# GpSimd's modulation units pause in parts of the last two layers, and three smaller edits on TensorE

## The chip, the cores and the metric

The kernel runs on one core of one Trainium2 chip. The metric is the device time of one execution in microseconds. TensorE's clock has two levels, 1.2 and 2.4 GHz; the profile shows the granted one as a share of the higher, so 0.50 is 1.2 GHz. All data is float32.

## What is computed

Two blocks of two layers each work on a sequence of 256 positions with 2048 features. The first block has a convolution and latent attention layer and a grouped attention layer. The second block, in which most of this change lies, is this, once for each of its two layers (cut to what matters):

```python
for l in range(2):
    shift, scale, gate = jnp.split(c_act @ w_ada[l] + b_ada[l], 3, axis=-1)
    h = rms_norm(x, norm_w[l]) * (1.0 + scale[:, None, :]) + shift[:, None, :]
    (gq, gk, gv, glr, gz, dq, dk, dv, da, db, dz, aq, ak, av, az) = jnp.split(h @ w_in[l], bounds, axis=-1)
    # gated linear attention, 4 heads of 64 key and 128 value features, in chunks of 64 positions
    att = jnp.where(causal, jnp.einsum('bhncd,bhnsd->bhncs', q_e, k_e), 0.0)
    o_gla = jnp.einsum('bhncs,bhnsv->bhncv', att, v) + jnp.einsum('bhncd,bhndv->bhncv', q_e, s_prev)
    # gated delta rule: its q, k and v pass a convolution over 4 positions first
    qkv = jax.nn.silu(causal_depthwise_conv(jnp.concatenate([dq, dk, dv], axis=-1), gdn_conv_w[l]))
    # differential attention, 8 query and 8 key maps of 128 features
    q_d = rms_norm(aq.reshape(B, S, 4, 2, 128), diff_q_norm_w[l])
    k_d = rms_norm(ak.reshape(B, S, 4, 2, 128), diff_k_norm_w[l])
    x = x + gate[:, None, :] * (jnp.concatenate([o_gla, o_gdn, o_diff], axis=-1) @ w_out[l])
```

The modulation vectors (shift, scale, gate) are products of one row with a matrix of 2048 x 6144 in each of the four layers; in the first block they are wanted for two rows, the input's and the context's.

## The kernel before

The large weights stream through the chip as 346 tiles of 128 output features by 2048 input features, 1 MB each. SyncE issues their loads (`load`, L724), four tiles ahead, into a ring of four buffers. Every tile is split into two parts for accuracy: ScalarE rounds it to an upper part (`upper`, L862), VectorE subtracts to get the lower part (`lower`, L1461), and TensorE then does 48 matmuls of 128x128 by 256 columns on it (`part_of_tile`, L2385): high by high, high by low, low by high, for each of 16 steps, in two halves of 8 steps. ScalarE copies the result out (L875).

The tiles are numbered through the whole program. The input tiles of layer 2, the first of the second block, are 194 to 253 (phase `s_in2`), its output tiles 254 to 269 (`s_out2`); layer 3 has 270 to 329 (`s_in3`) and 330 to 345 (`s_out3`). Between the phases stand the norms, which must be ready before the next tile can start. The small work of a layer (norms, linear attention, delta rule, differential attention) is written as one generator per engine; it is cut into pieces by slot numbers, two slots for a weight tile, and each piece stands in the engine's instruction order behind that half of a tile. Every engine works strictly in its order.

The tiles of `dq`, `dk` and `dv` have the convolution: for each, VectorE does one scaling (L2214) and three multiply-adds over 128x256 (L2216), besides the lower half of the weight tile.

The modulation vectors are worked out beside the weight tiles, in 80 blocks of 256 features. 24 blocks, 192 units, belong to TensorE: their pieces of weight go to three buffers (`load_gemv`), and `gemv_units` does them. A table, `GEMV_AT`, gives for each tile in the first block a list of up to three units: the first two of the list stand in the middle of the tile, a third behind it. Sixteen tiles have three. The other 56 blocks are GpSimd's, four units each. A unit is a load of 512 KB (`load_pool`, L722), which SyncE issues right behind the load of a weight tile, and six GpSimd instructions (L819 twice, L822, L826 or L828, L829). `pool_units_by(q)` gives how many units are issued by the load of tile q: two for every three tiles from tile 97 on. When a block is finished TensorE transposes its row (L2348), VectorE or ScalarE takes it in (`mod_event`), and `MOD_COLS_AT` gives the tile. `gains(l)` works out products of the scale vectors with the norm's weights.

Linear attention's outputs, at slot `gla_o`, are made head by head (L2751 and L2755): for one head four chunks, the first term with the full height of the array, the second with 64 rows, the lower half of the rows for one head of a pair and the upper half for the other. Even heads write bank G[2], odd ones G[3]. At slot `diff_qs`, TensorE sums the squares of the queries with 16 matmuls of one result column each (L2887), and those of the keys with `row_sums`, eight matmuls that leave their sums as rows (L2554).

## Time and profile before

| | us |
|---|---|
| Median of three runs | 2895.1 |
| The three runs | 2896.65, 2884.96, 2895.1 |
| The profiled execution | 2885.66 |
| Its span | 2882.8 |
| TensorE busy | 2724.0 (94%) |
| VectorE busy | 1739.1 (60%) |
| ScalarE busy | 1208.2 (42%) |
| GpSimd busy | 1476.2 (51%) |
| Mean granted TensorE clock | 0.969 |

### The profile page before, as it was taken

The numbers are of one execution on the slowest core, as the hardware profiler recorded it, in microseconds if no ns is written. First come the engines' busy times: TensorE is split into PE (matmuls) and PEld (weight loads), VectorE is DVE, ScalarE is ACT, GpSimd is POOL, SyncE is SP. The second block draws the span as 40 slices with busy tenths as digits, with TensorE's granted clock in tenths as the row PEclk, the third lists the DMA queues.
The fourth block names the chain that finished last, engine by engine and source line by source line (L and its number), as shares of the span: only waits on it lengthen the run. The fifth ranks groups of instructions, "written<-read, shape, count | busy, mean of one in ns | idle before, by whom it ended". The sixth has DMA issues, their size and how long they took to land.

```text
span 2882.8 us, 51276 instructions
## 1 busy us (share of the span) xinstructions
PE 2724.0 (94%) x22179; PEld 2516.7 (87%) x22179; DVE 1739.1 (60%) x1903; ACT 1208.2 (42%) x1438; POOL 1476.2 (51%) x1071
## 2 busy tenths in 40 slices
PE   5799999999999999999999969899999898999999
PEld 2488888888888899889989959899899798999999
DVE  2343544654554658686677665965766658745753
ACT  1233444333333334344575364532453445434442
POOL 0056766976676787665436826544548754400000
PEclk8799999999999999999999979999999998999999
DMA  9998998998887988776556837755668676644465
GB/s 337 292 309 254 275 265 243 290 285 246 242 240 227 288 246 225 202 208 183 156 142 187 236 95 189 208 153 140 176 163 219 184 198 172 165 112 122 121 164 155
DMA packets 948768, 599.21 MB, mean 208 GB/s; under 512 B 22070, under 2 KB 945088, under 8 KB 948032
## 3 DMA queue, kind: packets, MB, share of 16 engines
q1 hardware_dynamic: 944720, 582.83, 72.3%
q10 hardware_dynamic: 3824, 13.11, 1.2%
q8 instruction: 175, 2.87, 0.4%
q14 instruction: 49, 0.40, 0.0%
HBM read 589.46 MB, written 6.29 MB: 207 GB/s over the span
## 4 chain that ended last, share of the span: by engine, by line
PE 74%; DVE 12%; DMA 6%; ACT 3%; POOL 2%; issue 2%; SPq 1%; DVEq 0%; ACTq 0%; POOLq 0%
PE G L2385 55%; DMA ring<-in_w_mod_dram 3%; DVE ring_r L1461 3%; PE A L2325 2%; DMA const<-in_w_mod_dram 1%; DVE S L2216 1%; PE A L2447 1%; PE A L2453 1%; POOL ring L819 1%; PE A L2450 1%; PE G L2469 1%; PE A L2488 1%; ACT ring_r L862 1%; PE G L2824 1%; PE A L2836 1%
## 5 line engine op out<-in xcount | busy, mean ns | idle before, releaser
L2385 PE MATMUL G<-H_r,ring_r 128*128 128x256 f32 x10032 | 1706.6, 287 | 54.0 <-DVE S_r L1450 19.7
L2385 PEld LDWEIGHTS G<-H_r,ring_r 128*128 128x128 f32 x10032 | 1476.5, 191 | 90.1 <-issue 61.2
L819 POOL TENSOR_TENSOR ring<-ring,act_in 128x512 f32<-128x512 f32 x448 | 673.2, 1523 | 979.5 <-DMA ring<-in_w_ada_dram 736.6
L1461 DVE TENSOR_TENSOR ring_r<-ring,ring_r 128x2048 fp32r<-128x2048 f32 x346 | 860.7, 2488 | 287.3 <-ACT ring_r L862 286.2
L862 ACT ACTIVATE ring_r<-ring 128x2048 fp32r<-128x2048 f32 x346 | 661.6, 1912 | 325.7 <-PE G L2385 104.0
L2385 PE MATMUL G<-M_r,ring_r 128*128 128x256 f32 x4528 | 788.9, 284 | 0.0
L2385 PEld LDWEIGHTS G<-M_r,ring_r 128*128 128x128 f32 x4528 | 643.8, 189 | 12.0 <-issue 11.4
L2385 PE MATMUL G<-S_r,ring_r 128*128 128x256 f32 x1920 | 550.3, 287 | 0.0
L2385 PEld LDWEIGHTS G<-S_r,ring_r 128*128 128x128 f32 x1920 | 373.9, 195 | 3.4 <-issue 3.4
L822 POOL TENSOR_TENSOR ring<-ring 128x512 f32<-128x512 f32 x224 | 362.0, 1616 | 17.6
L828 POOL TENSOR_TENSOR ring<-ring 128x256 f32<-128x256 f32 x168 | 204.1, 1215 | 13.2
L829 POOL TENSOR_TENSOR mod_rows<-mod_rows,ring 128x256 f32<-128x256 f32 x168 | 183.3, 1091 | 13.2
L875 ACT ACTIVATE S<-G 128x256 f32<-128x256 f32 (+1 forms) x138 | 52.9, 384 | 282.3 <-PE G L2385 282.1
L2325 PE MATMUL A<-const,act_in 128*32 128x256 f32 x768 | 73.6, 394 | 13.4 <-DMA const<-in_w_mod_dram 12.9
L1680 DVE SCALAR_TENSOR_TENSOR X<-G,mod,X 128x256 f32<-128x256 f32 x80 | 38.4, 481 | 68.4 <-PE G L2385 67.9
L875 ACT ACTIVATE M<-G 128x256 f32<-128x256 f32 x72 | 27.4, 381 | 102.9 <-PE G L2385 102.9
L2295 PE MATMUL G<-ring,act_in 128*32 128x256 f32 x512 | 46.6, 527 | 23.4 <-DMA ring<-in_w_mod_dram 23.4
L1504 DVE TENSOR_REDUCE small<-G 128x2 f32<-128x256 f32 x44 | 18.5, 421 | 76.5 <-PE G L2348 76.3
L875 ACT ACT_TABLE_LOAD x43 | 55.2, 1283 | 19.3 <-PE G L2385 18.6
L2216 DVE SCALAR_TENSOR_TENSOR S<-M,pcol,S 128x256 f32<-128x256 f32 x72 | 59.8, 831 | 2.6
L1580 DVE TENSOR_REDUCE small<-G 128x1 f32<-128x256 f32 (+1 forms) x32 | 17.7, 554 | 69.2 <-PE G L2473 69.2
L1113 ACT ACTIVATE E<-G,small 128x512 f32<-128x512 f32 x32 | 24.9, 779 | 75.9 <-DVE small L1784 75.8
(440 smaller groups left out, 2611.9 us busy)
## 6 DMA issues: line engine op xcount, KB each, us to landing
ring<-in_w_in_dram SPq DMA_DIRECT2D x120, 1024.0 KB, 5.7
ring<-in_a_w_in_dram SPq DMA_DIRECT2D x98, 1024.0 KB, 7.0
ring<-in_w_ada_dram SPq DMA_DIRECT2D x192, 512.0 KB, 6.8
const<-in_w_mod_dram SPq DMA_DIRECT2D x192, 256.0 KB, 5.5
ring<-in_c_w_in_dram SPq DMA_DIRECT2D x48, 1024.0 KB, 5.8
ring<-in_w_mod_dram SPq DMA_DIRECT2D x16, 2048.0 KB, 18.0
ring<-in_a_w_out_dram SPq DMA_DIRECT2D x32, 1024.0 KB, 6.5
ring<-in_w_out_dram SPq DMA_DIRECT2D x32, 1024.0 KB, 5.9
```

Source lines behind the costliest of these rows:

```text
L819: g.mark(pool.tensor_tensor(w[:, i:i + 2, :], w[:, i:i + 2, :], act_in[:, k:k + 2, c:c + 1].broadcast_to((P, 2, BW)), ALU.mult))
L822: g(pool.tensor_tensor(w[:, 0:2, :], w[:, 0:2, :], w[:, 2:4, :], ALU.add))
L828: g(pool.tensor_tensor(w[:, 0, :], w[:, 0, :], w[:, 1, :], ALU.add))
L829: ins = pool.tensor_tensor(total, total, w[:, 0, :], ALU.add)
L862: act.activation(w_up(tl), w_raw(tl), ACT.Copy).then_inc(w_hi, 1)
L875: act.activation(dst, G[tl.bank][0:rows, 0:SEQ], func).then_inc(bank_free[tl.bank], 1)
L1461: v.tensor_tensor(w_low(tl), w_raw(tl), w_up(tl).bitcast(F32), ALU.subtract).then_inc(w_lo, 1)
L1680: v.scalar_tensor_tensor(out=x[:, j, :], in0=G[tl.bank][:, 0:SEQ], scalar=mod[:, gate:gate + 1], in1=x[:, j, :], op0=ALU.mult, op1=ALU.add ...
L2216: ins = v.scalar_tensor_tensor(out=CA[:, j % 2, :], in0=src, scalar=w, in1=CA[:, j % 2, :], op0=ALU.mult, op1=ALU.add)
L2295: ins = pe.matmul(G[2 * (b % 2)][o:o + 32, 0:BW], act_in[:, k, :], wide(b % 4)[:, k, :], start=(k < 4), stop=(k >= KT - 4))
L2325: ins = pe.matmul(A[3][o:o + 32, 0:BW], act_in[:, k, :], gemv_unit(m)[:, i, :], start=(k < 4), stop=(k >= KT - 4), skip_group_check=True)
L2385: ins = pe.matmul(G[tl.bank][:, 0:SEQ], w, x, start=(k == 0 and n_ == 0), stop=(k == KT - 1 and n_ == 2))
```

## The change

1. `pool_units_by` leaves out the load tiles in `PAUSED`: in each of the two layers those from four tiles ahead of its first input tile to one behind it, and those of the tiles 9 to 24. The rate in other tiles is 18 for every 25 instead of 2 for 3, and the last unit's load stands with tile 328 instead of 298. Through the later blocks, `gains(3)` moves behind output tile 11 of layer 2.
2. The sums of squares of the queries are made with `row_sums` as rows of 256, the root, reciprocal and scaling work on 128x256, and two transposes and a copy bring them into the former place.
3. Linear attention's outputs are looped over pairs of heads, positions and then the two heads of the pair.
4. `gemv_units` does the whole list in the middle of the tile.

```diff
+PAUSED = [FIRST[_name][0] + _j for _name in ("s_in2", "s_in3") for _j in [*range(-4, 2), *range(9, 25)]]
 def pool_units_by(q):
     first = max(0, min(q, 97) - 7)
-    return min(POOL_UNITS, first + 2 * max(0, q - 97) // 3)
+    working = max(0, q - 97) - sum(97 < p <= q for p in PAUSED)
+    return min(POOL_UNITS, first + 18 * working // 25)
...
-                    take_root(f"diff_q{l}", small[:, 32:48])
+                    take_root(f"diff_q{l}", df["q_rows"])
...
-                    ask_root(f"diff_q{l}", small[:, 32:48], G[3][:, 0:16], 1.0 / P)
-                    V(v.reciprocal(small[:, 32:48], small[:, 32:48]))
-                    V(v.tensor_scalar(small[:, 32:48], small[:, 32:48], P ** -0.5, None, ALU.mult))
+                    q_rows = df["q_rows"]
+                    ask_root(f"diff_q{l}", q_rows, G[3][:, 0:SEQ], 1.0 / P)
+                    V(v.reciprocal(q_rows, q_rows))
+                    V(v.tensor_scalar(q_rows, q_rows, P ** -0.5, None, ALU.mult))
...
                     after_p("diff_bc", l)
+                    turned_q = G[3][:, SEQ:2 * SEQ].rearrange("p (t g x) -> p t g x", t=2, g=4)
+                    V(v.tensor_copy(small[:, 32:48].rearrange("p (t g r) -> p t g r", t=2, g=4), turned_q[:, :, :, 0:2]))
...
-                if l == 2:
-                    gains(3)
                 for j in range(16):
...
                     mod_event(FIRST[f"s_out{l}"][0] + j)
+                    if l == 2 and j == 11:
+                        gains(3)
...
-                gemv_units(GEMV_AT.get(q, [])[0:2])
+                gemv_units(GEMV_AT.get(q, ()))
...
-                        else:
-                            gemv_units(GEMV_AT.get(q, [])[2:])
...
-                    for h in range(GLA_H):
-                        p, b, o = h // 2, h % 2, 64 * (h % 2)
-                        for c in range(NCH):
-                            t = c // 2
-                            if c % 2 == 0:
+                    for p in range(2):
+                        for t in range(2):
+                            for b in range(2):
+                                h = 2 * p + b
                                 pe.matmul(G[2 + b][:, p * SEQ + t * P:p * SEQ + (t + 1) * P], GV[:, t, h * P:(h + 1) * P],
...
+                            for c in range(max(1, 2 * t), 2 * t + 2):
+                                for b in range(2):
+                                    o = 64 * b
+                                    ins = pe.matmul(G[2 + b][:, p * SEQ + c * CHUNK:p * SEQ + (c + 1) * CHUNK],
...
-                    for j in range(8):
-                        for t in range(2):
-                            ins = pe.matmul(G[3][:, t * 8 + j:t * 8 + j + 1], df["sq_q"][:, j, t * P:(t + 1) * P], ones[:, 0:1],
-                                            start=(j == 0 and t == 0), stop=True, skip_group_check=True)
+                    ins = row_sums(None, [(j // 2, j % 2, df["sq_q"][:, j, :]) for j in (0, 2, 4, 6, 1, 3, 5, 7)], G[3], SEQ)
...
+                    for t in range(2):
+                        pe.transpose(G[3][:, SEQ + t * P:SEQ + (t + 1) * P], df["q_rows"][:, t * P:(t + 1) * P], ident)
```

SyncE's order in layer 3 before, where the convolution tiles' weights are loaded; `in_w_in` is a weight tile, `in_w_ada` a GpSimd unit's piece:

```order
L722 DMA ring<-in_w_ada_dram 128x4x256
L729 DMA ring<-in_w_in_dram 128x16x128
L722 DMA ring<-in_w_ada_dram 128x4x256
L729 DMA ring<-in_w_in_dram 128x16x128 x2
L722 DMA ring<-in_w_ada_dram 128x4x256
```

The same stretch in the changed kernel, from the last loads of layer 2's output tiles on:

```order
L734 DMA ring<-in_w_out_dram 128x16x128 x4
L734 DMA ring<-in_w_in_dram 128x16x128 x4
L727 DMA ring<-in_w_ada_dram 128x4x256
L734 DMA ring<-in_w_in_dram 128x16x128
L727 DMA ring<-in_w_ada_dram 128x4x256
L734 DMA ring<-in_w_in_dram 128x16x128
L727 DMA ring<-in_w_ada_dram 128x4x256
L734 DMA ring<-in_w_in_dram 128x16x128 x2
L727 DMA ring<-in_w_ada_dram 128x4x256
L734 DMA ring<-in_w_in_dram 128x16x128
L727 DMA ring<-in_w_ada_dram 128x4x256
L734 DMA ring<-in_w_in_dram 128x16x128 x18
```

A unit's load behind every tile or every second one is gone from two stretches, of 8 and of 18 weight loads.

TensorE's order at the linear attention outputs before, the first two heads; G2 and G3 are the banks, E and H the inputs of the first term, X and S those of the second:

```order
L2751 MATMUL G2<-E,H 128x128
L2755 MATMUL G2<-X,S 128x64
L2751 MATMUL G2<-E,H 128x128
L2755 MATMUL G2<-X,S 128x64 x2
L2751 MATMUL G3<-E,H 128x128
L2755 MATMUL G3<-X,S 128x64
L2751 MATMUL G3<-E,H 128x128
L2755 MATMUL G3<-X,S 128x64 x2
```

And in the changed kernel, the same two heads:

```order
L2756 MATMUL G2<-E,H 128x128
L2756 MATMUL G3<-E,H 128x128
L2762 MATMUL G2<-X,S 128x64
L2762 MATMUL G3<-X,S 128x64
L2756 MATMUL G2<-E,H 128x128
L2756 MATMUL G3<-E,H 128x128
L2762 MATMUL G2<-X,S 128x64
L2762 MATMUL G3<-X,S 128x64
L2762 MATMUL G2<-X,S 128x64
L2762 MATMUL G3<-X,S 128x64
```

The same matmuls stand in another order, with the bank changing at each one, and fewer changes between the two terms.

TensorE's order at the first modulation units before; L2325 is a unit of the modulation, two instructions each, L2385 the weight tile:

```order
L2325 MATMUL A<-const,act_in 32x256 x4
L2385 MATMUL G<-H_r,ring_r 128x256 x24
L2325 MATMUL A<-const,act_in 32x256 x2
L2385 MATMUL G<-H_r,ring_r 128x256 x24
L2325 MATMUL A<-const,act_in 32x256 x4
L2385 MATMUL G<-H_r,ring_r 128x256 x24
L2325 MATMUL A<-const,act_in 32x256 x2
L2385 MATMUL G<-H_r,ring_r 128x256 x24
```

And in the changed kernel, where the lines are L2333 and L2393:

```order
L2333 MATMUL A<-const,act_in 32x256 x6
L2393 MATMUL G<-H_r,ring_r 128x256 x48
L2333 MATMUL A<-const,act_in 32x256 x6
L2393 MATMUL G<-H_r,ring_r 128x256 x48
L2333 MATMUL A<-const,act_in 32x256 x4
```

The third unit, which stood between two tiles, has moved half a tile forward.

## Rows read from the trace of the kernel before

**Rows 1.** The page's list of busy times and their share of the span.
```profile
PE 2724.0 (94%) x22179; PEld 2516.7 (87%) x22179; DVE 1739.1 (60%) x1903; ACT 1208.2 (42%) x1438; POOL 1476.2 (51%) x1071
```
**Rows 2.** Timeline of TensorE in a weight tile: start us, length us, instruction.
```profile
2480.09 0.28 PE L2385 MATMUL G<-S_r,ring_r 128*128 128x256 f32 x1
...
2480.80 0.28 PE L2385 MATMUL G<-S_r,ring_r 128*128 128x256 f32 x1
```
**Rows 3.** Windows: length, busy time of five engines, clock, DMA share, GB/s.
```profile
1786.00:1872.00 86.00, 78.28 (x659) 75.39 (x658) 79.26 (x79) 47.11 (x55) 42.63 (x36) 0.98 0.79 212
2386.00:2480.00 94.00, 83.87 (x686) 81.13 (x685) 83.02 (x80) 49.72 (x57) 51.48 (x38) 0.95 0.72 191
```
**Rows 4.** TensorE's waits from 1780 to 1870: total us, times, longest.
```profile
PE G L2385 <- ACT M L875: 3.3, 1, 3.3
PE G L2348 <- ACT M L875: 2.5, 1, 2.5
PE G L2385 <- DVE mod L1436: 1.9, 2, 1.7
```
**Rows 5.** TensorE's waits from 2390 to 2480.
```profile
PE G L2385 <- DVE mod L1441: 5.6, 2, 3.2
PE G L2385 <- ACT M L875: 4.6, 1, 4.6
```
**Rows 6.** Timeline of VectorE in the convolution tiles of layer 3.
```profile
2441.27 2.29 DVE L1461 TENSOR_TENSOR ring_r<-ring,ring_r 128x2048 fp32r<-128x2048 f32 x1 [1.79 <-ACT ring_r L862]
...
2443.86 1.53 DVE L2216 SCALAR_TENSOR_TENSOR S<-M,pcol,S 128x256 f32<-128x256 f32 x3
...
2453.82 3.13 DVE L1461 TENSOR_TENSOR ring_r<-ring,ring_r 128x2048 fp32r<-128x2048 f32 x1
...
2458.04 3.23 DVE L2216 SCALAR_TENSOR_TENSOR S<-M,pcol,S 128x256 f32<-128x256 f32 x3
```
**Rows 7.** TensorE at the linear attention outputs: timeline, then a clock window.
```profile
1742.43 1.16 PE L2721 MATMUL G<-X 64*128 64x128 f32 x16
...
2372.13 0.39 PE L2751 MATMUL G<-E,H 128*128 128x128 f32 x2
...
2379.44 1.11 PE L2755 MATMUL G<-X,S 64*128 64x64 f32 x4
...
2377.40:2384.20 6.80, 6.80 (x28) 0.50 0.00 0
```
**Rows 8.** Query norms: TensorE and VectorE timelines, then a clock window.
```profile
2642.98 3.63 PE L2887 MATMUL G<-ones,H 128*128 128x1 f32 x32
...
2654.95 1.14 PE L2685 MATMUL A<-S,const 32*128 32x256 f32 x16
...
2458.82 1.07 PE L2554 MATMUL A<-E,small 128*32 128x256 f32 x16
...
2649.84 1.75 DVE L1920 RECIPROCAL S<-S 128x256 f32<-128x256 f32 x1 [0.55 <-ACT S L1198]
...
2647.00:2650.50 3.50, 3.50 (x24) 0.51 0.32 76
```
**Rows 9.** Modulation units: TensorE's timeline, the page's group and DMA line.
```profile
566.56 0.79 PE L2325 MATMUL A<-const,act_in 128*32 128x256 f32 x8
...
570.31 0.63 PE L2325 MATMUL A<-const,act_in 128*32 128x256 f32 x4
...
L2325 PE MATMUL A<-const,act_in 128*32 128x256 f32 x768 | 73.6, 394 | 13.4 <-DMA const<-in_w_mod_dram 12.9
...
const<-in_w_mod_dram SPq DMA_DIRECT2D x192, 256.0 KB, 5.5
```
**Rows 10.** Windows over the same stretch of layer 2 and of layer 3.
```profile
1891.70:2181.60 289.90, 285.07 (x2297) 271.86 (x2295) 190.66 (x219) 118.99 (x157) 141.68 (x106) 0.98 0.62 166
2497.10:2780.10 283.00, 280.54 (x2287) 268.03 (x2285) 166.07 (x209) 118.61 (x157) 5.38 (x5) 0.99 0.49 128
```

More of the change, by code:

```diff
@@ L651, in build @@
               "sq_k": M[:, 4096:6144].rearrange("p (j t) -> p j t", j=8), "rows8": S[:, 5120:5376],
+              "q_rows": S[:, 5376:5632],
               "P": [two(S[:, 0:512]), two(S[:, 512:1024])], "PT": [E[:, 0:256], E[:, 256:512]],
@@ L2753, in mixers @@
                                           skip_group_check=True)
-                            if c:
-                                ins = pe.matmul(G[2 + b][:, p * SEQ + c * CHUNK:p * SEQ + (c + 1) * CHUNK],
-                                                gla["st"][o:o + 64, c - 1, p * P:(p + 1) * P],
-                                                qe[o:o + 64, p, c * CHUNK:(c + 1) * CHUNK], start=False, stop=True,
-                                                skip_group_check=True)
+                            for c in range(max(1, 2 * t), 2 * t + 2):
+                                for b in range(2):
+                                    o = 64 * b
+                                    ins = pe.matmul(G[2 + b][:, p * SEQ + c * CHUNK:p * SEQ + (c + 1) * CHUNK],
+                                                    gla["st"][o:o + 64, c - 1, p * P:(p + 1) * P],
+                                                    qe[o:o + 64, p, c * CHUNK:(c + 1) * CHUNK], start=False, stop=True,
+                                                    skip_group_check=True)
                     PS.done(ins, "gla_o")
```

## The prediction

> **What bounds the kernel now.** I read the page's list of busy times first. TensorE is busy 94% of the span, VectorE 60%, ScalarE 42% and GpSimd 51% [rows 1]. So VectorE and GpSimd cost time only where TensorE waits for them, and an instruction of TensorE costs its full length wherever it stands. Between two of TensorE's own instructions there is hardly room: six matmuls of a weight tile start within 0.71 us (2480.80 − 2480.09), 0.118 each, so a tile of 48 takes 5.68 us [rows 2]. That number is the allowance for every other engine: whatever ScalarE or VectorE does for one tile must fit into 5.68 us, or TensorE waits.
>
> Next I read the windows over the convolution tiles of the last two layers, the waits inside them, and VectorE's timeline there. In 1786:1872 TensorE is busy 78.28 of 86.00 us, in 2386:2480 83.87 of 94.00, while VectorE is busy 92% and 88% of these windows, far above its 60% in the mean [rows 3]. TensorE's largest waits there are 3.3, 2.5 and 1.9 us in the first window (7.7) and 5.6 and 4.6 us in the second (10.2) [rows 4, 5]. The reader should see VectorE's two lengths for the same work: the lower half of a weight tile takes 2.29 us and three conv taps 1.53 us at 2441, but 3.13 and 3.23 us at 2454 [rows 6]. From the start of the first to the end of the taps that is 4.12 us against 7.45: under the allowance without GpSimd beside it, over it with GpSimd.
>
> The last views are small places: TensorE's timeline at the linear attention outputs, at the query norms and at a modulation unit in the first layers [rows 7 to 9], and the windows that compare a long stretch of the last two layers with and without GpSimd [rows 10].
>
> All sums below are made against the profiled execution, 2885.7 us, whose span is 2882.8; the 2.9 outside stay. It lies 9.4 below the median of the three runs, 2895.1, and close to the fastest, 2885.0.
>
> **1. GpSimd pauses in the conv tiles.** The order of SyncE's loads shows 18 weight loads in a row without a modulation load in layer 3 (before: one after every one or two tiles), so GpSimd has nothing to work on in the conv tiles. What can go: in the first window the waits, 7.7, and the part of the clock, 86 × (1 − 0.98) = 1.7, together 9.4; in the second 10.2 and 94 × (1 − 0.95) = 4.7, together 14.9. Sum 24.3. What may stay: the waits put down to ScalarE's result copies (L875), 3.3 + 2.5 + 4.6 = 10.4, if they are not VectorE's lateness passed on; then the gain is 13.9. I round the ends to 12 and 24. Per tile VectorE falls from 7.45 to 4.12 of 5.68, so 1.5 us a tile are free and the backlog cannot build up; the delta rule's norms in the same tiles keep single VectorE operations that no pause shortens. I take −21, near the upper end, since the rows with the long waits are the covered ones.
>
> A rule of the Trainium skill bears on this (SBUF — State Buffer, section "Who interferes with whom"): a VectorE instruction with two SBUF inputs contends with a GpSimd instruction that reads SBUF, one with a single SBUF input outside the two-port modes does not. The two instructions of rows 6 have two SBUF inputs and stretch by 0.84 and 1.70 us, so the trace agrees. The rule alone would make all of VectorE's excess go, the upper end of the term; the sum goes by the waits of the rows.
>
> In the norm ahead of layer 3's inputs the pause does nothing: the first paused load there is ordered behind one issued when the tile before the norm is done, as before. In the norm ahead of layer 2 there is now one unit where there was none. These go into part 6.
>
> **2. Linear attention outputs in head pairs.** Now the 40 passes lie between 2372.13 and 2380.55, 8.4 us, and from 2377.4 on the granted clock is 0.50 for 6.8 us, that is 1.2 GHz [rows 7]. At full clock the block would be 5.3 (to 2377.4) + 3.2 / 2 = 6.9 us. It holds 16 passes over the full height and 24 over half, of some 0.11 each, 4.4, which leaves 2.5 for the 16 turns between the two shapes, 0.15 each. Layer 2 shows the same and stands for nothing new. After the change the two heads alternate, on different rows of the array (0 and 64) and in different banks: 16 full passes, 12 pairs of half passes and 8 turns. The nearest row for alternating halves is L2721, 16 passes of 64 rows in 1.16 us, 0.07 each [rows 7], so a pair may cost as little as one pass: 28 × 0.11 + 8 × 0.15 = 4.3 us. Gain 2.6 at full clock; with the dip gone it is 8.4 − 4.3 = 4.1, and 1.8 on the weight tile behind, 5.9. If nothing overlaps and only the turns halve, it is 8 × 0.15 = 1.2 and some of the dip, 2.5. I take −3.5 a layer, nearer the row of full clock, −7 for two (−5 to −11).
>
> The rule against it is in the Trainium skill (TensorEngine Tiling (Array Packing), section "Gotcha 1: PSUM Pressure"): different row tiles cannot use the same PSUM bank at once. Here the pair uses banks 2 and 3, so the rule leaves the overlap; were both heads in one bank, it would take away 12 × 0.11 = 1.3 us a layer. No row of before shows such a pair in one bank.
>
> **3. Query norms as rows.** The sixteen matmuls with one column of results each (32 passes in the row) take 3.63 us in layer 3; the same kind of sum as rows takes 1.07 (L2554 over 128x256) [rows 8]. That is −2.6. Behind them the granted clock is 0.51 for 3.5 us, 1.2 GHz, some 1.7 us lost [rows 8], most of which should go with the stretch of one-column work ahead of it. TensorE gets two more transposes, 2 × 0.12. Net −4 us on TensorE, and layer 2 alike. VectorE pays: its reciprocal becomes the 1.75 us one of 128x256 [rows 8], the other steps on the same rows grow too, some 2 us in all, but its chain starts 2.5 earlier. TensorE wants the chain's end at L2685, 2654.95; the last reciprocal ended at 2651.59, 3.4 us ahead [rows 8]. When TensorE comes 4 us sooner and the chain half a microsecond sooner, that slack is just used up, so I take −3.5 a layer, −7 (−5 to −9).
>
> **4. A list of modulation units in one go.** In the first layers TensorE works up to three units per tile, by the table of lists: two in the middle of the tile take 0.79, one after it 0.63 [rows 9]. A unit beside another adds 0.79 − 0.63 = 0.16, so each of the 16 lists of three saves 0.47: 7.5 us. Against it: the third unit is wanted half a tile, 2.8 us, sooner, its load is issued only when a buffer comes free, a load takes 5.5 us from issue to landing against 5.68 + 0.79 between two lists, and TensorE already waits 12.9 us for these loads [rows 9]. I take −5, with −7 and +10 as ends.
>
> **5. The paused units come back in the last layer.** The last unit moves from tile 298 to tile 328, under the delta rule and the attention. The two windows are the same work in the two layers: with GpSimd (106 instructions) 289.90 us, without 283.00 [rows 10]. Of the 6.9, 2.9 are the clock (0.98 against 0.99); VectorE is busy 24.59 us more and TensorE passes on little. About three quarters of such a stretch is now covered, and what I count as caused by it is +3, with 0 and +8 as ends.
>
> The rule of part 1 speaks for more here, since most of the delta rule's adds have two SBUF inputs: it makes VectorE's 24.6 us likely, but the rows say that TensorE sees a quarter at most. Taken at full length it is rival B.
>
> **6. The rest.** The denser rate (0.72 units a tile instead of 0.67), one unit in the norm ahead of layer 2, the later gains of layer 3 and two blocks whose transposes are put off past value tiles: +2 (−1 to +6). Each has the slack of VectorE behind a tile as cover; without it, a unit covers some 5 us of VectorE's work and lengthens it by at most the 3.33 of rows 6.
>
> **Sum.** −21 − 7 − 7 − 5 + 3 + 2 = −35; 2885.7 − 35 = 2850.7. A median lies a little above such a fast execution; half of the 9.4 is 4.7: 2855.
>
> **Rivals.**
> A: the conv tiles stay bound by something else, the ScalarE copies or the norms' own chain. For it: three of the five waits end on L875. Against it: ScalarE is busy 55% there [rows 3]. The gain is 12 and not 21: 2864.
> B: the moved units cost the last layer all of VectorE's 24.6 us instead of 3. For it: VectorE's chain feeds the delta rule's small matmuls. Against it: rows 10. It gives 2855 + 21.6 = 2877.
> A and B together: 2886, no change within what a measurement can tell, which for this kernel is about 0.5%, 14.5 us.
> C, slower: the third unit of the 16 lists waits for its load in the middle of a tile, and ScalarE's and VectorE's ring buffers behind it come free as much later. Without term 4 the sum is −30, so the kernel gets slower than before from 30/16 = 1.9 us a list on. At 3 us a list it is +48 − 30 = +18, 2903.7, with the median 2908. For it: the lists of three come in pairs (tiles 8 and 9, 19 and 20, ...), and the second of a pair must load all three in the 6.5 us between lists, at 5.5 a load. Against it: three loads can be under way together, and the present waits are 12.9 us over 192 units.
> D: the clock dips in 2 and 3 stay, since idle-looking short matmuls remain. Of the −14 some 6 would then be missing: 2861, inside the forecast's own range.
>
> **Chances.** Forecast (D within it) 0.58, own range 2844 to 2866; A 0.16; B 0.10; A and B together 0.10; C 0.06. Faster by over 0.5% (under 2880.6) in forecast, A and B: 0.84. Same: 0.10. Slower by over 0.5%: 0.06. The range reaches down to 2836, where the clock gives all and moved units cost nothing (−24 − 11 − 9 − 7 + 0 − 1 = −52 is the very end, 2834), and up to 2880 to hold B.
>
> **What would show it.** The windows of the two conv stretches: GpSimd near 0, TensorE's idle below 3 us in each, VectorE's lower halves all 2.29 us. If TensorE still waits for L875 there, A is right. The linear attention block at 5 us or less with no 0.50 window behind it; if it is 7 us, the halves do not overlap. One-column matmuls gone and L2554's successor 1.1 us long. TensorE's wait for the modulation units' DMA at 13 to 20 us in the whole run; above 45 C is right. In the stretch from the delta rule to the end of layer 3's inputs 286 us instead of 283; above 295 B is right. The forecast is wrong if the conv stretches keep over 10 us of the 24.3, or if the last stretch gives back more than 10.

## The result, and the profile after

| | before | after |
|---|---|---|
| Median of the runs, us | 2895.0 (4 runs) | 2865.1 (4 runs) |
| Range of the runs, us | 2885.0 to 2896.7 | 2861.2 to 2866.2 |
| Ratio, 95% interval | | 0.9904, 0.9888 to 0.9919 |
| Profiled execution, us | 2885.7 | 2864.2 |
| Its span, us | 2882.8 | 2862.3 |

The kernel became 1.0% faster, some 28 us. The forecast was 2855 with a range of 2836 to 2880. The time is also that of the prediction's rival A, 2864, so only the traces can tell the two apart.

The page of the changed kernel, with the list of busy times, GpSimd's slices, the group of the modulation units and their loads:

```profile
PE 2705.6 (95%) x22151; PEld 2503.6 (87%) x22151; DVE 1738.4 (61%) x1905; ACT 1209.2 (42%) x1438; POOL 1491.9 (52%) x1071
...
POOL 0056766986666788777455604054548440445420
...
L2333 PE MATMUL A<-const,act_in 128*32 128x256 f32 x768 | 71.0, 394 | 14.1 <-DMA const<-in_w_mod_dram 13.1
...
const<-in_w_mod_dram SPq DMA_DIRECT2D x192, 256.0 KB, 5.4
```

GpSimd's slices show what was moved: a 0 at 1.8 ms and another at 2.4 ms, the convolution tiles of the two layers, and work in the last slices, where [rows 10] had nearly none. TensorE waits 13.1 us for the modulation units' loads, as before [rows 9].

The windows over the same work as [rows 3], in the same columns (length, then the busy time of TensorE, its weight loads, VectorE, ScalarE, GpSimd, the clock):

```profile
1776.00:1864.00 88.00, 88.00 (x762) 85.03 (x761) 64.46 (x82) 53.29 (x61) 4.78 (x5) 1.00 0.67 174
2374.00:2451.00 77.00, 77.00 (x667) 74.78 (x666) 58.97 (x76) 48.48 (x55) 0.00 (x0) 1.00 0.71 185
```

TensorE is busy the whole time at full clock, and VectorE 73% and 77% instead of about 90%. The waits of [rows 4, 5] are all gone. VectorE's timeline answers to [rows 6]:

```profile
2406.96 2.28 DVE L1466 TENSOR_TENSOR ring_r<-ring,ring_r 128x2048 fp32r<-128x2048 f32 x1
...
2409.55 1.53 DVE L2224 SCALAR_TENSOR_TENSOR S<-M,pcol,S 128x256 f32<-128x256 f32 x3
```

The linear attention outputs on TensorE, in the order of the program, then the clock behind them; they answer to [rows 7]:

```profile
2365.99 0.61 PE L2756 MATMUL G<-E,H 128*128 128x128 f32 x4
2366.53 0.44 PE L2762 MATMUL G<-X,S 64*128 64x64 f32 x4
2366.90 0.71 PE L2756 MATMUL G<-E,H 128*128 128x128 f32 x4
2367.54 0.66 PE L2762 MATMUL G<-X,S 64*128 64x64 f32 x8
...
2369.78 0.66 PE L2762 MATMUL G<-X,S 64*128 64x64 f32 x8
...
2370.60:2377.40 6.80, 6.80 (x61) 1.00 0.43 115
```

The block takes 4.4 us (2365.99 to about 2370.4) instead of 8.4, and the next 6.8 us run at 2.4 GHz instead of 1.2. Eight half-height passes, 2367.54 to 2368.13, take 0.59 us. Four took the same before, 2376.79 to 2377.38, at the same clock:

```profile
2376.79 0.66 PE L2755 MATMUL G<-X,S 64*128 64x64 f32 x4
2377.38 0.79 PE L2751 MATMUL G<-E,H 128*128 128x128 f32 x2
```

The query norms, TensorE's timeline, answer to [rows 8]:

```profile
2616.06 1.07 PE L2560 MATMUL G<-H,small 128*32 128x256 f32 x16
2616.95 1.05 PE L2560 MATMUL G<-M,small 128*32 128x256 f32 x16
...
2624.72 0.44 PE L2899 MATMUL G<-const,S 128*128 128x128 f32 x2 [0.85 <-DVE S L1925]
2625.09 1.15 PE L2691 MATMUL A<-S,const 32*128 32x256 f32 x16
```

A list of three modulation units, TensorE's timelines, two rows of the kernel before and one of the changed kernel:

```profile
655.41 0.64 PE L2325 MATMUL A<-const,act_in 128*32 128x256 f32 x8
659.40 0.63 PE L2325 MATMUL A<-const,act_in 128*32 128x256 f32 x4
652.43 1.06 PE L2333 MATMUL A<-const,act_in 128*32 128x256 f32 x12
```

From its start to that of the next instruction, two units took 0.57 us and the third, behind the tile, 0.56; three in one go take 0.99. So a list of three saves 0.14 us, and the 16 lists 2.2; the group's busy time fell from 73.6 to 71.0.

So in three of the four places the change did what was forecast, and more; at the modulation units it did less. Adding up the tiles in which these places lie gives 28 us for the convolution tiles, 11 for the linear attention, 5 for the tiles with modulation units and 10 at the query norms, 54 in all, but the two profiled executions differ by 20 at the end of the last tile. The other 34 have to be found. I compared the times from the end of one weight tile to the end of the next in both traces. The sum by stretches, in us, after less before:

| weight tiles | after − before | what stands there |
|---|---|---|
| 1 to 97 | −4.7 | modulation units on TensorE |
| 98 to 137 | +4.5 | waits at 102, 126 and 136 |
| 138 to 177 | −1.2 | |
| 178 to 193 | +6.5 | tile 185 alone +6.5 |
| 194 to 202 | +2.1 | norm and first tiles of layer 2 |
| 203 to 218 | −17.6 | convolution −12.0, linear attention −5.6 |
| 219 to 253 | +4.7 | tile 236 −5.7, 237 +1.5, 241 +3.7, 249 +6.0 |
| 254 to 278 | −0.5 | |
| 279 to 296 | −22.5 | convolution −16.6, linear attention −5.9 |
| 297 to 345 | +8.2 | tile 312 −4.1, 313 +1.3, 317 +4.4, 319 to 325 +4.5 |

Four new or longer waits stand behind 20.6 us of this, at tiles 185, 241, 249 and 317. The +4.5 of tiles 98 to 137 and the +2.1 of 194 to 202 lie within what executions of the same code differ by (see the experiments); the +4.5 of tiles 319 to 325 is there in every kernel with the late units in the last layer, and in none of the three without them (at most +0.4). The four are in the groups of TensorE's waits, in windows around tiles 185, 241, 249 and 317 (total us, times, longest):

```profile
PE G L2393 <- DVE X L1685: 5.1, 1, 5.1
...
PE G L2393 <- DVE M L2169: 6.1, 1, 6.1
...
PE A L2691 <- DVE S L1923: 4.6, 1, 4.6
...
PE G L2393 <- DVE M L2169: 5.6, 1, 5.6
```

Before, the first was 0.7, the second 3.0, the third not there and the fourth 2.1.

**Tile 185.** Here VectorE works out the rotary angles, twelve short operations on 128x256. Its timeline in the changed kernel:

```profile
1599.74 0.83 DVE L1838 CAST S<-S 128x256 f32<-128x256 int32 x1
1600.60 1.08 DVE L1839 TENSOR_SCALAR S<-S,const 128x256 f32<-128x256 f32 x1
...
1602.78 1.34 DVE L1842 TENSOR_SCALAR S<-S 128x256 f32<-128x256 f32 x1
1604.15 3.29 DVE L1844 SCALAR_TENSOR_TENSOR S<-S 128x256 f32<-128x256 f32 x3
1607.47 1.24 DVE L1845 TENSOR_SCALAR const<-S 128x256 f32<-128x256 f32 x1
1608.74 0.77 DVE L1846 TENSOR_SCALAR S<-S 128x256 f32<-128x256 f32 x1
...
1611.13 0.48 DVE L1685 SCALAR_TENSOR_TENSOR X<-G,mod,X 128x256 f32<-128x256 f32 x1
```

The angles take from 1599.7 to 1611.1, 11.4 us, more than two tiles' allowance with the lower halves beside them; before they took 7.0 (1601.1 to 1608.1). The denser rate had put two of GpSimd's units on this place, back to back from 1600.5 to 1610.2; before, GpSimd paused there from 1602.6 to 1605.7 for a load.

**Tile 249.** VectorE (L1923) is only the last in a chain. GpSimd's timeline shows its start:

```profile
2102.22 1.27 POOL L827 TENSOR_TENSOR ring<-ring 128x512 f32<-128x512 f32 x1
2129.61 0.73 POOL L831 TENSOR_TENSOR mod_rows<-ring 128x256 f32<-128x256 f32 x1 [26.11 <-PE G L2356]
```

and SyncE's and ScalarE's show the next two steps:

```profile
2130.37 0.37 SPq L727 DMA_DIRECT2D ring<-in_w_ada_dram  x1
2130.78 0.51 SPq L734 DMA_DIRECT2D ring<-in_w_in_dram  x1
...
2138.62 1.92 ACT L867 ACTIVATE ring_r<-ring 128x2048 fp32r<-128x2048 f32 x1 [4.99 <-DMA ring<-in_w_in_dram]
2140.56 1.28 ACT L1203 ACT_TABLE_LOAD   x1
```

GpSimd stood still for 26.11 us because its two row buffers were full: a block is only free when TensorE has transposed it (L2356), and no transposes are placed in the value tiles 238 to 245. A unit's load waits for GpSimd, and SyncE is in order, so the weight load behind it went out at 2130.78 and ScalarE waited 4.99 us for it, and VectorE and TensorE for ScalarE. The pause had moved a block's last unit from tile 238 to 239, one tile too late for its transposes to stand ahead of the value tiles.

**Tiles 241 and 317.** TensorE waits for the last rotary step (L2169, `rope7`). This wait was in the kernel before, 3.0 and 2.1 us. In tile 241 it is longer because TensorE now comes earlier and VectorE, with GpSimd beside it as before, does not as much. In tile 317 it is the moved units: without them the wait is 2.1 us, as before the change (see "The moved units left out").

### The profile page after: what moved, and what is told of

Same layout as the page of the kernel before. It is cut to its first block, busy times and chain, and to the rows that moved or that the text cites. A ratio compares the mean times of both kernels' runs of the same rounds, so it can differ in the third digit from the quotient of the medians.

```text
span 2862.3 us, 51222 instructions
## 1 busy us (share of the span) xinstructions
PE 2705.6 (95%) x22151; PEld 2503.6 (87%) x22151; DVE 1738.4 (61%) x1905; ACT 1209.2 (42%) x1438; POOL 1491.9 (52%) x1071
## 4 chain that ended last, share of the span: by engine, by line
PE 78%; DVE 11%; DMA 6%; ACT 3%; issue 1%; SPq 1%; POOL 0%; DVEq 0%; ACTq 0%; POOLq 0%
PE G L2393 58%; DMA ring<-in_w_mod_dram 3%; DVE ring_r L1466 3%; PE A L2333 2%; DMA const<-in_w_mod_dram 2%; PE A L2453 1%; PE A L2459 1%; PE A L2456 1%; PE G L2475 1%; PE A L2494 1%; ACT ring_r L867 1%; PE A L2638 1%; PE G L2831 1%; SPq L718 1%; DVE M L2169 1%
## 5 line engine op out<-in xcount | busy, mean ns | idle before, releaser
L2393 PE MATMUL G<-H_r,ring_r 128*128 128x256 f32 x10032 | 1700.5, 287 | 52.0 <-DVE S_r L1455 20.7
L2393 PEld LDWEIGHTS G<-H_r,ring_r 128*128 128x128 f32 x10032 | 1473.3, 191 | 84.2 <-issue 56.9
L824 POOL TENSOR_TENSOR ring<-ring,act_in 128x512 f32<-128x512 f32 x448 | 659.9, 1494 | 1159.2 <-DMA ring<-in_w_ada_dram 915.9
L1466 DVE TENSOR_TENSOR ring_r<-ring,ring_r 128x2048 fp32r<-128x2048 f32 x346 | 875.1, 2530 | 274.2 <-ACT ring_r L867 273.2
L2393 PE MATMUL G<-M_r,ring_r 128*128 128x256 f32 x4528 | 789.5, 284 | 0.0
L2393 PEld LDWEIGHTS G<-M_r,ring_r 128*128 128x128 f32 x4528 | 645.5, 190 | 10.0 <-issue 9.4
L2393 PE MATMUL G<-S_r,ring_r 128*128 128x256 f32 x1920 | 546.5, 285 | 0.0
L827 POOL TENSOR_TENSOR ring<-ring 128x512 f32<-128x512 f32 x224 | 366.5, 1636 | 17.6
L2393 PEld LDWEIGHTS G<-S_r,ring_r 128*128 128x128 f32 x1920 | 369.9, 193 | 3.4 <-issue 3.3
L833 POOL TENSOR_TENSOR ring<-ring 128x256 f32<-128x256 f32 x168 | 211.7, 1260 | 13.2
L834 POOL TENSOR_TENSOR mod_rows<-mod_rows,ring 128x256 f32<-128x256 f32 x168 | 201.4, 1199 | 13.2
L2333 PE MATMUL A<-const,act_in 128*32 128x256 f32 x768 | 71.0, 394 | 14.1 <-DMA const<-in_w_mod_dram 13.1
L831 POOL TENSOR_TENSOR mod_rows<-ring 128x256 f32<-128x256 f32 x56 | 51.3, 917 | 49.1 <-PE G L2356 44.8
```

The source lines that it names most:

```text
L824: g.mark(pool.tensor_tensor(w[:, i:i + 2, :], w[:, i:i + 2, :], act_in[:, k:k + 2, c:c + 1].broadcast_to((P, 2, BW)), ALU.mult))
L827: g(pool.tensor_tensor(w[:, 0:2, :], w[:, 0:2, :], w[:, 2:4, :], ALU.add))
L831: ins = pool.tensor_tensor(total, w[:, 0, :], w[:, 1, :], ALU.add)
L833: g(pool.tensor_tensor(w[:, 0, :], w[:, 0, :], w[:, 1, :], ALU.add))
L834: ins = pool.tensor_tensor(total, total, w[:, 0, :], ALU.add)
L1466: v.tensor_tensor(w_low(tl), w_raw(tl), w_up(tl).bitcast(F32), ALU.subtract).then_inc(w_lo, 1)
```

## Experiments

Runs here took between 4 and 12 executions each. All ratios are to the kernel before, on the same chip. Executions of one kernel spread by 10 us and more, so an interval is about ±5 us; differences smaller than that are read from the traces, tile by tile. In these, the waits in the first layers (tiles 8 to 10, 54 to 58, 102, 126, 136 and 137) differ by 1 to 4 us from one execution to the next, between kernels that are the same there. Tiles 98 to 137 took 260.9 to 266.9 us in the ten kernels with the denser rate there; the kernel before took 261.9. Tiles 194 to 202 took 98.4 to 100.5, and the kernel before 98.3. The tiles with the wait for `rope7` differ as well: tile 241 took 15.9 us in the changed kernel, but 13.2 in the one that only leaves out the units of load tiles 296 to 328.

**No pause.** The line of `pool_units_by` and the place of `gains(3)` as before.

```diff
-    working = max(0, q - 97) - sum(97 < p <= q for p in PAUSED)
-    return min(POOL_UNITS, first + 18 * working // 25)
+    return min(POOL_UNITS, first + 2 * max(0, q - 97) // 3)
```

> The changed kernel with the unit loads of before: two units for every three tiles, nothing paused, gains(3) at its old place. My theory, from the tile-by-tile comparison of the two traces: the pause took 28.6 us out of the convolution tiles and cost some 22 elsewhere (6.5 at tile 185, where the rotary angles are worked out, 6 at tile 249, where a weight load stands behind a unit's load, 4 in tiles 98 to 137, 6 in the last layer), so undoing it costs only 5 to 9 us: 2870 to 2874. The rival, the prediction's own sum (-21 + 3 + 2 = -16 for the pause) gives 2881. TensorE's waits in the conv tiles must be back, and tile 185 at 6 to 7 us.

Measured: 2863.8, ratio 0.9916 (0.9899 to 0.9933), against 0.9904 for the whole change. The pause is worth nothing that can be told. In the trace, TensorE's waits in the convolution tiles of layer 3 are back (window 2390:2470):

```profile
PE G L2392 <- DVE mod L1445: 5.9, 2, 3.6
PE G L2392 <- ACT M L879: 4.6, 1, 4.6
```

and tiles 203 to 218 and 279 to 296 are 29.2 us longer than in the changed kernel. The rest is 30.6 us shorter: tile 185 −7.3, tile 249 −6.0, tiles 312 to 329 −11.3, of it tile 317 −5.9. My expectation had the parts right; its 5 to 9 us lie inside what the ratios allow, 3.5 ± 7, and the prediction's 16 us do not.

**Old query norms** in the changed kernel.

```diff
-                    ins = row_sums(None, [(j // 2, j % 2, df["sq_q"][:, j, :]) for j in (0, 2, 4, 6, 1, 3, 5, 7)], G[3], SEQ)
+                    for j in range(8):
+                        for t in range(2):
+                            ins = pe.matmul(G[3][:, t * 8 + j:t * 8 + j + 1], df["sq_q"][:, j, t * P:(t + 1) * P], ones[:, 0:1], ...
```

The root, reciprocal and scaling go back to 16 columns too, and the two transposes and the copy go (not shown).

> The changed kernel with the query norms of before (sixteen one-column matmuls). My theory: the 4 to 6 us that rows save TensorE at the sums are given back at the wait for the rotary work (rope7), which VectorE sets, so the time stays within 2 us of the changed kernel's 2865, and the wait in tile 241 falls from 6.1 back to about 3. The rival, the prediction's term 3: 7 us slower, 2872.

Measured: 2870.5, ratio 0.9924 (0.9902 to 0.9947), inconclusive as a time. The trace decides. Against the changed kernel, tile 236 is 4.12 longer, 237 1.47 shorter and 241 3.51 shorter: 0.9 in favour of the old form; in layer 3 +4.12, −1.28 and −5.14, 2.3 in its favour. Of tile 241 up to 2.7 us are the spread named above: against 13.2 instead of 15.9 us, the rows are 1.9 us better in layer 2. The waits for `rope7`, in layer 2 and layer 3:

```profile
PE G L2390 <- DVE M L2166: 3.3, 1, 3.3
...
PE G L2390 <- DVE M L2166: 2.8, 1, 2.8
```

What the execution is longer by lies elsewhere, where the two kernels are alike: 7.5 us in tiles 307 to 309, whose small matmuls ran at the lower clock, and 2.9 in tiles 50 to 97. So in the changed kernel the query norms as rows bring nothing that can be told; most of what TensorE saves is handed over to the next two waits for VectorE. This does not hold where GpSimd is idle beside it. The kernel without the pause has no GpSimd unit in tiles 311 to 318, like the kernel before, and takes 61.0 us there against 65.8: all of what the rows save is kept, and the wait for `rope7` is 2.1 us in both.

**Old linear attention order** in the changed kernel (the loops head by head).

> The changed kernel with the linear attention outputs head by head as before. My theory, from the tiles 204 and 280 (15.8 and 16.0 us before, 10.2 both after): 11 us slower, 2876. The rival, the prediction's term 2: 7 us slower, 2872, if 4 of the 11 come from something else in these tiles.

Measured: 2872.7, ratio 0.9947 (0.9930 to 0.9964) against 0.9904, 12 ± 7 us; the medians are 7.6 apart. In the trace tiles 204 and 280 are 5.61 and 6.85 longer, 12.5. Tiles 241 and 317 are 4.6 shorter, but they are as short, 13.1 and 13.9 us, with the angles free of GpSimd, where linear attention is as in the changed kernel, so this need not come from the edit. The first theory holds in the tiles; the time alone does not tell it from the rival's 7 us.

**The wait for the last rotary step, later.** `rope7` is first needed by the scores at slot 96, but TensorE waited for it at slot 94, with a whole weight tile between.

```diff
-                    after_v("rope7", l)
                     for n_ in range(11):
                         yield SLOT["attn"] + n_
+                        if n_ == 0:
+                            after_v("rope7", l)
```

> The changed kernel with TensorE's wait for the last rotary step (rope7) moved from right behind the last rotation matmul (slot 94) to the first scores (slot 96), which are the first to need it. Theory: the waits of 6.1 and 5.6 us in tiles 241 and 317 are only this early wait; a tile of weights (5.7 us) now lies in between, so they fall below 1 us and with the clock that they cost the kernel gains 10 to 14 us: 2851 to 2855. The rival: VectorE is behind in all that follows too (lower halves, maxima), and the wait comes back at the scores or at the next lower half: no gain, 2862 to 2866.

Measured: 2851.8, ratio 0.9874 (0.9851 to 0.9897). Tiles 241 and 317 are 8.3 and 8.2 us shorter than in the changed kernel, more than the waits of 6.1 and 5.6, since behind a wait TensorE ran at the lower clock for a while. No wait for L2169 is left. By the ratios the kernel is 9 ± 8 us faster than the changed one; that it is the early wait is shown by the two tiles.

**Late wait with the old query norms.** The two edits above together.

> The late wait for rope7 together with the query norms of before. In e2 the old norms cost TensorE 4.12 us at the sums and were 1.5 and 3.5 to 5.1 us better at the next two waits. Theory: with the wait late, only the first two are left, so the old norms now cost 4.1 - 1.4 = 2.7 us a layer, some 5 us in all against the 2851.8 of the late wait alone: 2857. Rival: the norms' rows gain nothing even then, because VectorE is behind afterwards: 2852.

Measured: 2859.7, ratio 0.9897 (0.9876 to 0.9919), against 0.9874. In the traces tiles 236 and 237 are 4.16 − 1.45 longer and 312 and 313 4.15 − 1.28, together 5.6, and nothing is given back at 241 or 317. The theory holds in the traces; the times fit it, but their intervals meet. The query edit is worth some 5 us once the wait behind it is gone.

**Blocks ahead of the value tiles.** A table moves eight of the unit loads.

```diff
+MOVED = {238: 237, 239: 238, 310: 309, 311: 310, 312: 311, 314: 312, 315: 313, 316: 314}
```

> The changed kernel with eight unit loads one or two tiles earlier (238 and 239 to 237 and 238; 310 to 316 to 309 to 314), so that two blocks are complete before the value tiles, whose transposes hold back theirs. Theory: GpSimd's wait of 26 us for the transposes, and with it the late weight load at tile 249, was due to that: TensorE's wait of 4.65 us there goes, 6 us, and 2 to 3 more at tiles 319 to 321: 2856 to 2859. Rival: the late load comes from the many units crowded behind the pause, and another tile waits instead: 2865.

Measured: 2858.9, ratio 0.9894 (0.9877 to 0.9910). Tile 249 is 6.00 shorter, its wait of 4.65 is gone, and GpSimd's longest waits there are for loads, 12.4 and 11.0 us. At tiles 319 to 321 nothing was gained, and the rest came at tiles 241 and 317.

**Angles free of GpSimd.** Four unit loads moved behind tile 185.

```diff
+MOVED = {185: 188, 186: 189, 188: 190, 189: 191}
```

> The changed kernel with the four unit loads of tiles 185, 186, 188 and 189 moved to 188 to 191, so that GpSimd has nothing while VectorE works out the rotary angles in tile 185. Theory: the ten operations there took 11.4 us instead of 6 because GpSimd was busy beside all of them; TensorE's wait of 5.1 us in tile 185 goes and with its clock 6 to 7 us: 2858. Rival: VectorE was late at tile 185 for another reason (the gates' reads ahead of it), and the wait stays above 3 us: 2864.

Measured: 2858.8, ratio 0.9891 (0.9875 to 0.9908). Tile 185 takes 5.68 us instead of 13.10, without a wait. The theory holds.

**All three.**

> The changed kernel with the late wait for rope7, the blocks ahead of the value tiles and the angles free of GpSimd. Theory: the three act in different places and add up: -16 (tiles 241 and 317), -7 (tile 249 and 319 to 321), -6.5 (tile 185): 2865 - 29 = 2836. Rival: TensorE, now ahead, runs into other waits on VectorE or on loads that give a third back: 2845.

Measured: 2840.5, ratio 0.9826 (0.9805 to 0.9846). In the trace the tiles 185, 241, 249 and 317 are −7.42, −8.31, −6.00 and −8.21, 29.9 in all; the median is 4.5 us above the expected 2836. By the ratios the three are worth 22 ± 7 us, so the time doesn't tell the sum from the rival, which gives a third back. VectorE's angles, the same kind of operations as above, now beside an idle GpSimd:

```profile
1596.20 0.29 DVE L1854 TENSOR_SCALAR S<-S 128x256 f32<-128x256 f32 x1
1596.53 1.34 DVE L1856 SCALAR_TENSOR_TENSOR S<-S 128x256 f32<-128x256 f32 x3
1597.90 0.30 DVE L1857 TENSOR_SCALAR const<-S 128x256 f32<-128x256 f32 x1
1598.24 0.29 DVE L1858 TENSOR_SCALAR S<-S 128x256 f32<-128x256 f32 x1
```

**The moved units left out.** SyncE's loads and GpSimd's arithmetic of the last 24 units.

```diff
-                for m in range(pool_units_by(tl.q - 1), pool_units_by(tl.q)):
+                for m in range(pool_units_by(tl.q - 1), min(200, pool_units_by(tl.q))):
...
+                    if p >= 50:
+                        if u == 0:
+                            pool.wait_ge(pool_cols, p - 1)
+                        pool.memset(total[:, 0:1], 0.0).then_inc(pool_used, 1)
```

> The changed kernel without the loads and the arithmetic of GpSimd's last six blocks (the 24 units of load tiles 296 to 328), so the last gates are not computed; transposes and their reads stay. It prices the units that the pause put into the last layer. Theory: in the changed kernel tiles 311 to 329 take 143.5 us against 132.2 without GpSimd there (e1); without the units they take 132 to 134, of it 3 to 4 at tile 317 and 3 at 319 to 321: 10 us less, 2855. Rival: the prediction's +3, 2862.

Measured: 2853.9, ratio 0.9872 (0.9851 to 0.9892), 9 us less than the changed kernel. Tiles 312 to 329 take 132.8 instead of 143.5. The windows over them, of the changed kernel and of this one, and the wait at tile 317 of this one:

```profile
2640.00:2759.00 119.00, 109.38 (x866) 104.05 (x865) 87.27 (x107) 55.14 (x87) 53.88 (x38) 0.97 0.63 168
```

```profile
2640.00:2749.00 109.00, 106.55 (x868) 101.50 (x866) 71.25 (x104) 54.71 (x87) 0.40 (x4) 1.00 0.56 145
...
PE G L2399 <- DVE M L2175: 2.1, 1, 2.1
```

VectorE's busy time falls by 16 us and TensorE's stretch by 10.6. The moved units cost three times what was forecast or more, 5.85 of it at the one wait of tile 317 (3.9 against the 13.9 us that this tile took with the angles free). What is left of that wait is 2.1 us, the 2.1 of the kernel before, although the query norms bring TensorE there some 4 us sooner.

**Late wait without the pause.** The edits of the first and the fourth experiment together.

> The late wait for rope7, with the unit loads of before (nothing paused). Theory: in the changed kernel the pause's 29 us were used up by tile 185 (7), tile 249 (6), tiles 98 to 137 (7), the last layer (11, of it 4 at tile 317). The late wait takes away only the last 4, so the pause is now worth some 4 us, and this kernel takes 2852 + 4 = 2856; compared with its own version without the late wait (e1, 2863.8) it gains 2 x 2 to 3 for the waits and their clock, 8. Rival: it gains the same 13 to 16 as the late wait did on the paused kernel: 2849.

Measured: 2864.7, ratio 0.9909 (0.9894 to 0.9925). Both expectations missed it. In the trace tiles 241 and 317 are 8.39 and 2.37 shorter than without the late wait, 10.8 together where the first theory has 8, but 6.1 us are lost before tile 129 and 2.6 in tiles 203 to 218, in places that the edit does not touch. I can't say whether a run of these kernels would show the 8 us; what stays open is the execution's own spread. What can be told is the comparison with all three: 0.9826 against 0.9909, 24 ± 7 us; in the traces tiles 203 to 218 and 279 to 296 differ by 30.7. With the collisions removed, the pause keeps most, if not all, of what it takes out of the convolution tiles.

**The rate of before up to tile 190.** As all three, with two units for three tiles first, and four more units at tiles 248, 252, 255 and 259.

> As e9 (late wait, blocks ahead, angles free), but with the rate of before, two units for three tiles, up to tile 190, and the four units that this leaves over at tiles 248, 252, 255 and 259. Theory: the denser rate cost 4 to 7 us in tiles 98 to 137 (tiles 102, 126, 136); they come back, and four more units under the delta rule's and the output tiles' slack cost 1: 2840.5 - 4 = 2836. Rival: the waits at 102 and 126 change by 2 us from one execution to the next and have nothing to do with the rate: 2840.

Measured: 2854.6, ratio 0.9865 (0.9843 to 0.9888): 14 us slower than all three by the medians and 11 ± 9 by the ratios, so the theory is wrong twice. Tiles 98 to 137 are 3.5 us longer and not shorter, with the waits at 102 and 126 as in the others: they do not come from the rate. And with one unit in every tile from 246 to 261 these tiles take 11.2 us more. The waits of TensorE from 2080 to 2240 in this kernel:

```profile
PE G L2365 <- ACT S L882: 6.5, 4, 2.7
PE G L2395 <- DVE M_r L1457: 5.8, 4, 3.1
PE A L2358 <- POOL mod_rows L836: 3.9, 2, 2.1
```

TensorE now comes to the transposes before GpSimd has the row.

**Key rows first.** As all three, with VectorE's scaling of the queries behind the key rows.

```diff
-                    step(VS, v.tensor_scalar(QD, QD, prm("diff_q_norm_w_2", L), None, ALU.mult), "diff_q", l)
                     head_rows(no + 4, f"diff_k{l}", df["rows8"], G[2][:, 0:SEQ], 1.0 / P)
+                    step(VS, v.tensor_scalar(QD, QD, prm("diff_q_norm_w_2", L), None, ALU.mult), "diff_q", l)
```

> As e9, with VectorE's scaling of the queries by their norm weight (1.71 us) moved behind the root and reciprocal of the key rows. The rows that the query edit put on VectorE made TensorE wait 1.70 us for the key rows in tile 237 and 1.51 in tile 313. Theory: these waits fall below 0.3 us each, with their clock 4 us less in the two tiles together: 2836.5. Rival: the scaling then delays VectorE's next step, which TensorE wants as much, and the time stays at 2840.5.

Measured: 2837.4, ratio 0.9818 (0.9799 to 0.9837). The waits at 237 and 313 are down from 1.70 and 1.51 to 0 and 0.14, and these tiles 3.44 and 1.37 shorter, 4.8 together. As a time it can't be told from all three. It has the lowest median of all kernels here, 1.8% below the kernel before.

## Why the prediction came out as it did

The time lies inside the range and the direction is right, but the sum of −35 was not what happened: the tiles aimed at gained 54 us instead of 40, and 34 were given back instead of 5. Of these 20.6 lie in four tiles, of which the prediction had named the cause of one. That the time still lay only 10 us from the forecast is luck: the two errors have opposite signs.

**Part 1, the convolution tiles: right, too small.** −28.6 in place of −21 (tiles 203 to 218 without 204, 279 to 296 without 280). The upper end, 24.3, was counted from waits and clock inside two windows; tiles beside them gained too. The waits put down to ScalarE went with the others, as the alternative of lateness passed on had it, and rival A is out, although its 2864 is the time that was measured.

**Part 2, linear attention: right, too small.** −5.6 and −5.9 in place of −3.5 each, and 12 ± 7 us by the third experiment. The working by passes gave 4.3 us for the block and it took 4.4, and with the clock behind it 5.9 a layer; I chose a value below my own working. The Trainium skill's rule (TensorEngine Tiling (Array Packing), "Gotcha 1: PSUM Pressure") left room for this overlap since the banks differ, and the trace agrees: eight half-height passes in the time of four. No run here put the pair into one bank.

**Part 3, query norms: the step that failed.** I let VectorE's chain end at L2685, where 3.4 us of slack were to be used up, and took −7. TensorE did come 5.7 and 4.1 us sooner (1.6 of the 5.7 is not the edit's: with the old norms in the changed kernel the tile is 4.1 longer in both layers), and lost 1.5 and 1.3 at that place, where half a microsecond was forecast. But the next wait for VectorE, `rope7` at tiles 241 and 317, had 3.0 and 2.1 us before the change already, and I did not look at it. The net is −0.5 in layer 2 and +1.5 in layer 3 together with the moved units; the late wait with the old query norms shows 5.6 us for the edit once that wait is moved. In layer 3 the loss comes from part 5: with GpSimd idle in these tiles, as in the kernel before, the rows are worth 4.8 us (61.0 against 65.8 in tiles 311 to 318), more than the 3.5 forecast. So the two terms were not independent, and the prediction added them as if they were.

**Part 4, modulation units: too large.** I read that a unit beside another adds 0.16 us, from a row of 0.79 that was not typical: 74 of the 88 lists of two took 0.57 us to the next instruction. The third unit adds 0.42, so the 16 lists save 2.2 us in place of 7.5. The −4.7 of tiles 1 to 97 looks like the forecast −5, but this stretch took 841.7 to 847.9 us in the thirteen kernels with this edit, on average 2.6 less than in the one trace before. No experiment takes this edit back. The wait for loads is 13.1 us against 12.9, and rival C is out.

**Part 5, the moved units: too small.** 10.6 in place of +3, beyond the upper end of 8 and, if only just, beyond the 10 that the prediction itself called the sign of being wrong; by the ratios it is 9 ± 7. The stretch of tiles 296 to 329, for which it had 286 us, took 291.1, below the 295 of rival B. The two windows of [rows 10] compared stretches of both layers as wholes, in which much of what GpSimd costs VectorE is hidden; the part with the rotary steps, where VectorE sets the end, was not looked at by itself. It is not rival B either, which takes all of VectorE's time: 16 us more on VectorE gave 10.6.

**Part 6, the rest: the second step that failed.** +2, at most +6, was forecast. Tile 185 (+6.5) and tile 249 (+6.0) alone are 12.5. The two blocks with late transposes were in the list, but their price was taken as VectorE's slack; what decided was a queue: GpSimd full, a unit's load waiting for it, a weight load behind that on SyncE. The angles were not in the list at all. The rule that costs were bounded by, a unit lengthening VectorE's work by at most 3.3, was right in size (4.4 at the angles, for two units), but there was no slack to cover it.

**The sum of the two halves.** The pause, for which parts 1, 5 and 6 gave −16, is worth 0 within the intervals: the kernel without it is as fast. Most of the 28 us, 24 by its ratio, comes from the edits that shorten TensorE's own work, and in its trace linear attention is 11.2 of 21.8.

## What to carry to other kernels

When work is moved off a busy stretch, list what stands where it goes, tile by tile, and which instruction there is already waited for; the mean over a long window hides it. A gain ahead of an existing wait is kept only as far as the engine that is waited for comes sooner too; here that was all of it with GpSimd idle, and at most half with GpSimd beside VectorE. So search for the waits behind the gain before pricing it, and check that each of them stands at the first use and not earlier. In a program with in-order queues, a helper engine that is blocked for a buffer holds up everything that is queued behind its loads.

## What the runs showed of the hardware

Of VectorE's operations here, the short one with one input suffered most beside GpSimd. A `tensor_scalar` over 128x256 took 0.29 us with GpSimd idle and 0.77 to 1.34 beside it, up to four and a half times as long; three `scalar_tensor_tensor` took 1.34 and 3.29, and the lower half of a tile, eight times as large, 2.29 and 3.13. The Trainium skill (SBUF — State Buffer, "Who interferes with whom") says that a `tensor_scalar` in a two-port mode and a GpSimd instruction lock each other out for whole instructions. By that rule short operations lose the most in proportion, since each can wait for one long one of GpSimd, and the trace agrees: they lost 0.5 to 1.05 us each, and one instruction of GpSimd takes 0.7 to 1.3.

A long wait of TensorE costs more than its length. Removing waits of 6.1 and 5.6 us shortened their tiles by 8.3 and 8.2, and removing one of 5.1 shortened its tile by 7.4: the granted clock was 0.50, 1.2 GHz, for over 4 us behind each. A wait of 2.1 us cost only 2.4 (tile 317, 9.99 us with it and 7.62 without). The windows behind the three, of the changed kernel (length, TensorE busy, clock, DMA share, GB/s):

```profile
2079.50:2084.00 4.50, 4.46 (x21) 0.50 0.00 0
2665.10:2669.60 4.50, 4.50 (x21) 0.50 0.00 0
1611.80:1616.00 4.20, 4.20 (x20) 0.50 0.40 120
```
